# A gated delta rule's block inverse on one core: trimmed join products, and the second coupling as 32-column products in a packed operand

## The reference

```python
gc = jnp.cumsum(g, axis=-1)
decay = jnp.exp(jnp.where(causal, gc[..., :, None] - gc[..., None, :], -jnp.inf))
kb = k * beta[..., None]
a = jnp.where(strict, jnp.einsum('bhnid,bhnjd->bhnij', kb, k) * decay, 0.0)
rhs = jnp.concatenate([v * beta[..., None], kb * jnp.exp(gc)[..., None]], axis=-1)
sol = lax.linalg.triangular_solve(a + eye, rhs, left_side=True, lower=True)
u, w = sol[..., :dv], sol[..., dv:]
qk = jnp.where(causal, jnp.einsum('bhnid,bhnjd->bhnij', q, k) * decay, 0.0)
def step(state, inp):
    v_new = u_c - jnp.einsum('bhcd,bhde->bhce', w_c, state)
    o = jnp.einsum('bhcd,bhde->bhce', qd_c, state) + jnp.einsum('bhij,bhje->bhie', qk_c, v_new)
    state = state * cd_c[..., None, None] + jnp.einsum('bhcd,bhce->bhde', kd_c, v_new)
```

## Time and profile before

| | |
|---|---|
| Median of 3 runs | 2663.14 us (2659.54 to 8724.83) |
| The profiled execution's own time | 2661.84 us |
| Its span on the core | 2660.1 us |
| PE busy | 2594.3 us, 98% |
| Weight loads (PEld) | 2153.7 us, 81% |
| DVE busy | 1637.7 us, 62% |
| POOL busy | 1180.7 us, 44% |
| ACT busy | 1116.7 us, 42% |
| DMA, mean | 89 GB/s |
| TensorE's granted clock, mean | 0.995 |

### The profile page before, as it was taken

How to read it: one execution, slowest core, us unless ns; L and a number is a source line. 1 busy time by engine, 2 the same in 40 slices (tenths; PEclk the granted TensorE clock), 3 DMA queues, 4 the chain that set the end, 5 groups by cost and what they waited for, 6 DMA issues and landing times. The chain is left out here.

```text
span 2660.1 us, 34055 instructions
## 1 busy us (share of the span) xinstructions
PE 2594.3 (98%) x12821; PEld 2153.7 (81%) x12821; DVE 1637.7 (62%) x1743; ACT 1116.7 (42%) x1648; POOL 1180.7 (44%) x721
## 2 busy tenths in 40 slices
PE   7899999999999999999999999999999999999998
PEld 5788888888878888888888788888878888888887
DVE  5677666676177666665455657557557666665454
ACT  6445545545353443433344334434533434343242
POOL 2444333435313878774443111112413887874442
PEclk9999999999999999999999999999999999999999
DMA  3111011102342222224554111012521222224453
GB/s 121 30 43 47 32 41 46 47 32 73 95 146 78 87 72 96 72 95 159 180 173 137 58 32 48 24 55 70 166 98 64 87 84 84 80 99 155 171 189 115
DMA packets 84540, 238.06 MB, mean 89 GB/s; under 512 B 8928, under 2 KB 22816, under 8 KB 84416
## 3 DMA queue, kind: packets, MB, share of 16 engines
q1 hardware_dynamic: 84416, 236.39, 26.8%
HBM read 189.66 MB, written 46.69 MB: 89 GB/s over the span
## 5 line engine op out<-in xcount | busy, mean ns | idle before, releaser
L398 POOL TENSOR_TENSOR f_wlo<-f_raw,f_whi 128x512 fp32r<-128x512 f32 (+1 forms) x210 | 427.6, 2037 | 490.1 <-ACT f_whi L439 490.1
L712 DVE TENSOR_TENSOR f_hlo<-f_hraw,f_hhi 128x512 fp32r<-128x512 f32 x88 | 182.9, 2084 | 198.9 <-ACT f_hhi L497 198.9
L439 ACT ACTIVATE f_whi<-f_raw 128x512 fp32r<-128x512 f32 (+1 forms) x210 | 172.0, 834 | 269.2 <-PE f_value L82 252.2
L398 POOL TENSOR_TENSOR f_wlo<-f_sums,f_whi 128x512 fp32r<-128x512 f32 x144 | 188.5, 1319 | 39.8 <-ACT f_whi L439 39.8
L439 ACT ACTIVATE f_whi<-f_sums 128x512 fp32r<-128x512 f32 x144 | 90.4, 627 | 271.2 <-POOL f_sums L404 271.2
L80 PE MATMUL f_value<-x_hi,f_whi 128*128 128x512 f32 x416 | 162.7, 391 | 1.2 <-POOL f_wlo L398 1.2
L81 PE MATMUL f_value<-x_lo,f_whi 128*128 128x512 f32 x416 | 162.6, 391 | 0.0
L82 PE MATMUL f_value<-x_hi,f_wlo 128*128 128x512 f32 x416 | 162.5, 391 | 0.0
L80 PE MATMUL f_part<-f_whi,f_hhi 128*128 128x512 f32 x352 | 137.9, 392 | 0.0
L82 PE MATMUL f_part<-f_whi,f_hlo 128*128 128x512 f32 x352 | 137.5, 391 | 0.0
L81 PE MATMUL f_part<-f_wlo,f_hhi 128*128 128x512 f32 x352 | 137.1, 389 | 0.0
(11 more groups left out here) (539 smaller groups left out, 7649.0 us busy)
## 6 DMA issues: line engine op xcount, KB each, us to landing
f_raw<-in_ffn_w_up SPq DMA_DIRECT2D x88, 512.0 KB, 3.6
f_raw<-in_ffn_w_down SPq DMA_DIRECT2D x88, 512.0 KB, 3.6
hidden<-f_hid SPq DMA_DIRECT2D x44, 512.0 KB, 2.7
f_hraw<-hidden SPq DMA_DIRECT2D x88, 256.0 KB, 4.0
g_raw_first<-in_gdn_w_in SPq DMA_DIRECT2D x16, 512.0 KB, 3.6
g_raw<-in_gdn_w_in SPq DMA_DIRECT2D x16, 512.0 KB, 4.2
f_xt<-x_mid SPq DMA_DIRECT2D x16, 512.0 KB, 4.8
l_raw_first<-in_gla_w_in SPq DMA_DIRECT2D x12, 512.0 KB, 3.5
```

Source lines behind the costliest of these rows:

```text
L398: pool.tensor_tensor(part_of(w_lo, k), source, part_of(w_hi, k).bitcast(F32), ALU.subtract) \
L439: act.activation(part_of(w_hi, k), source, ACT.Copy).then_inc(s_hi, 1)
L712: dve.tensor_tensor(h_lo[d % FFN_SLOTS][:, :], h_raw[d % HIDDEN_RAWS][:, :], plain32(h_hi[d % FFN_SLOTS][:, :]), ALU.subtract).then_inc(s_ ...
```

## The change

Four things change, all in the joins.

- Join 0: `joined(0)` makes only 96 of the 128 rows of the inverse (`kept_rows`; the last 32 are needed by no later product), so its weight has 96 columns instead of 128, and DVE subtracts on 96 partitions. The moving operand keeps its 128 columns.
- Join 1, coupling: `coupled(1)` made 8 products of 128x128. It now makes 16 of 32x32 with 96 rows of contraction, one for each of the two pairs of 32-blocks (`PAIRS`), both in partitions 0 to 31 of `pm`. ACT copies them with 4 copies of 32x128 elements instead of 2 of 128x512, to the places (b, b) of `m1_low`, a view on `rowsT` of 64 columns for each chunk. What is between has to be zero, so POOL clears `m1_low` once per head (128x512), ahead of `coupling(h, 1)`; ACT waits for it on a new semaphore.
- Join 1, the join: `joined(1)` made 16 products of 128 columns with weights of 128 columns. It now makes 8 with weights of 64 columns and 32 moving columns, and 8 with weights of 64 columns and 64 moving columns. DVE's `join(1)` had 2 subtractions of 128x512 per half; it now has 3 of 32x128.
- Join 2: `coupled(2)` contracts over 64 rows instead of 128; its weight keeps 128 columns and its moving operand 64.

```diff
+        m1_low = rowsT[:, :].rearrange("p (c t) -> p c t", c=NT)
...
+        QUARTER = P // 4
+        PAIRS = [(slice(2 * b * QUARTER, (2 * b + 1) * QUARTER), slice((2 * b + 1) * QUARTER, (2 * b + 2) * QUARTER),
+                  slice(b * QUARTER, (b + 1) * QUARTER)) for b in range(2)]
+        kept_rows = slice(0, 3 * QUARTER)
...
                 spread(h, 1)
+                pool.memset(m1_low, 0.0).then_inc(s_zero, 1)
                 coupling(h, 1)
...
                     act.wait_ge(s_m1p, 2 * J * h + 2 * n + a + 1)
+                    if 0 < n < J - 1:
+                        if a == 0:
+                            act.wait_ge(s_zero, h + 1)
+                        for _, down, packed in PAIRS:
+                            last = act.activation(m1_low[down, part, packed],
+                                                  by_chunk(pm)[0:QUARTER, part, packed], ACT.Copy)
+                        last.then_inc(s_m1, 1)
+                        continue
...
-                    was, wasT = (inv, invT) if n else (first, firstT)
-                    dve.tensor_tensor(inv[:, part, :], was[:, part, :], x[:, 0], ALU.subtract)
-                    dve.tensor_tensor(invT[:, part, :], wasT[:, part, :], x[:, 1], ALU.subtract).then_inc(s_t, 1)
+                    if n:
+                        up, down, _ = PAIRS[0]
+                        dve.tensor_tensor(inv[down, part, up], inv[down, part, up], x[down, 0, :, up], ALU.subtract)
+                        for up, down, packed in PAIRS:
+                            last = dve.tensor_tensor(invT[up, part, down], invT[up, part, down],
+                                                     x[packed, 1, :, packed], ALU.subtract)
+                        last.then_inc(s_t, 1)
+                        continue
+                    dve.tensor_tensor(inv[kept_rows, part, :], first[kept_rows, part, :], x[kept_rows, 0],
+                                      ALU.subtract)
+                    dve.tensor_tensor(invT[:, part, :], firstT[:, part, :], x[:, 1], ALU.subtract).then_inc(s_t, 1)
...
                         if n == J - 1:
-                            last = pe.matmul(out[:, low], cT[:, c, :], x[:, c, low], start=True, stop=True)
+                            last = pe.matmul(out[:, low], cT[low, c, :], x[low, c, low], start=True, stop=True)
+                        elif n:
+                            for up, down, packed in PAIRS:
+                                last = pe.matmul(out[0:QUARTER, packed], cT[kept_rows, c, down],
+                                                 x[kept_rows, c, up], start=True, stop=True)
                         else:
-                            last = pe.matmul(out, (cT if n else near_cT)[:, c, :], x[:, c, :], start=True, stop=True)
+                            last = pe.matmul(out, near_cT[:, c, :], x[:, c, :], start=True, stop=True)
...
-                        pe.matmul(pt[:, at:at + P], xT[:, i, :], m1[:, i, :], start=True, stop=True)
+                        if n:
+                            pe.matmul(pt[low, at:at + QUARTER], xT[:, i, low], m1_low[:, i, 0:QUARTER],
+                                      start=True, stop=True)
+                            out = pt[low, at + HALF:at + HALF + P // 2].rearrange("p (b t) -> p b t", b=2)
+                            lower = xT[:, i, :].rearrange("p (b half t) -> p b half t", b=2, half=2)[:, :, 1, :]
+                            last = pe.matmul(out, m1_low[:, i, :], lower, start=True, stop=True)
+                            continue
+                        pe.matmul(pt[kept_rows, at:at + P], xT[:, i, kept_rows], m1[:, i, :], start=True, stop=True)
```

More of the change, by code:

```diff
@@ L1575, in gdn @@
         s_ct, s_m1p, s_m1 = sem("coupling_made"), sem("coupling_product_done"), sem("coupling_product_copied")
+        s_zero = sem("coupling_rows_zeroed")
         s_x, s_t = sem("join_products_done"), sem("blocks_joined")
```

## The result

The change makes the kernel slower: 2690.02 us in the median of four runs (2689.34 to 2691.81), against 2661.63 us for the kernel before on the same chip. The ratio is 1.0112, with a 95% interval of [1.0096, 1.0128]; it leaves out before's one slow run of 8724.83 us, without which before's median is 2660.12. So the change costs 30 us (28 against the median with that run), where I had expected 8 us less. I had forecast 2654, with a range up to 2664.

A forecast was written before the change was run, and what follows sets the result against it. PE bounds the kernel, with the gain capped by the start of DVE's second join. Seven heads at 0.96 us plus 1.5 for head 0 sum to 8.2 us, giving 2654 us; its own range 2651 to 2658, overall range 2648 to 2664.

The forecast's parts named there:

- The bound: PE, busy 98% of the span, counts; in front of the third coupling DVE's second join, starting at 339.96, caps the gain.
- the price of a narrow record: In `coupled(1)`, 0.067 us per record of a 32-column weight (bounds 0.033 and 0.118), making it 0.33 us longer.
- the line: Record price drawn through 0.113 us at 128 weight columns and 0.067 at 64, giving 0.044 at 32.
- rival B: `coupled(1)` ends early, POOL's `coupling(2)` precedes DVE's second tap, join 1.9 us later; 0.9 per head lost, 2668 us; chance 0.12.
- the proportion: Record cost going on in proportion to weight width: 0.033 us at 32 columns, half of 0.067.
- head 0: No fills there: `joined(1)` 1.35 us shorter, the 0.54 wait mostly gone, `coupled(1)` 0.33 longer; gain taken as 1.5 us.
- `joined(1)`: PE's products for join 1: 32 records with 64-column weights at 0.067, 2.14 us instead of 3.49.
- The third coupling: `coupled(2)` on PE: two halves of 0.92 us plus 0.1 for 32-row products and shape change, ending at 342.71 instead of 343.67.
- rival C: Array shape changes in `prepare` cost 0.3 us per border, not 0.09: 3 us in all, time 2658; chance 0.08.
- rival A: Narrow records cost 0.118 us: `coupled(1)` takes 3.78, 0.2 per head lost, time 2663.6; chance 0.12.
- DVE's pieces: Small subtractions of DVE's `join(1)`: 0.275 us each, neighbours overlapping by 0.08, three taking 0.67.
- Case D: `coupling(2)` lets DVE's third tap go first, so the join starts earlier: 1.4 us per head gained, 2651 us; chance 0.05.

## Why the prediction was wrong

**The bound.** That PE counts and that the join's start caps the gain was right, and it is what went wrong: the cap itself moved. I had its distance from the start of `coupled(1)` as constant, 8.3 us; it became 351.56 - 341.83 = 9.7.

**The step that failed: the price of a narrow record.** I took 0.067 us for a 32-column record, "since 64 columns already cost more than half of 128". It measured 1.13 / 32 = 0.035, next to the lower bound of 0.033 and below the line's 0.044. The floor of about 62 ns that the Trainium skill, TensorE: Matmul & The Clock Gate, section on 56 ns and 53.3 ns, gives for matmuls decoded by microcode is not what bounds these records; the other of its two, about 25 ns, is not contradicted. I had put the point where rival B decides at 0.047, and gave B 0.12 all the same. (Even that point was too low by my own numbers: over by 333.3 from a start at 331.64 is 1.66 / 32 = 0.052.) With both ends of the bound in hand and the deciding point between them, the chance of B had to follow from where in 0.033 to 0.118 the value may lie; two of the three ways to read it (the line and the proportion) lay on B's side.

**Rival B's size.** The mechanism was as written, in this order: POOL ahead of the second tap, two taps slowed, the join late. The join came 1.40 us later, where I had 1.9, and cost 0.72 per head with the clock up, where I had 0.9. B's 2668 counted seven such heads and a gain of 1.5 in head 0; the run with the wait filled measured 2672.9, with six such heads and losses in head 0, in the last head and behind it.

**The other step that failed, and the larger: the clock was in no case.** I let PE's idle time cost its own length. It cost 2.98 us per head on top of the join's 0.72, and six times 2.98 is 17.9 of the 30 us; from after to the run with the wait filled the time fell by 17.2 (2690.02 to 2672.86). The page of before showed a clock of 0.995 in the table, and I did not ask what holds it there. My range up to 2664 had no room for it. The kernels with the flip removed (2676, 2666, 2661) are above it or in its upper part for the same reason.

**The other terms.** `joined(1)`: 346.56 - 344.55 = 2.01, forecast 2.14. The third coupling, both halves with the shape changes: 1.97 with the clock up, forecast 1.94 (two halves and 0.1 for the changes), so rival C falls; rival A fell with the narrow record. DVE's pieces measured 0.28 each, as forecast, but don't overlap: three take 352.42 - 351.56 = 0.86, not 0.67. Over two halves that is 0.2 to 0.4 us, about the difference between the forecast's gain of 0.96 per head and what a head without a flip or a fall gained, 78.23 - 77.54 = 0.69; no run tested it alone. The MEMSET (0.52) costs nothing, as said; ACT's copies (four in 1.11 us, as forecast) lie under fill 20 in the loop. I had counted seven heads like head 3; head 7 is not one (67.58 us to its end in before). Head 0 was wrong in sign: a gain of 1.5 was forecast, and the stretch from its `coupled(1)` on became 2.2 us longer. ACT comes to its copies there only 3.01 us behind the start of `coupled(1)` (102.87 - 99.86), as in before (102.15 - 99.26 = 2.89), so what the narrow products save PE waits for, and behind that wait the clock falls for 10.2 us. With the waits filled the stretch is back at 74.88, against 74.59. The forecast's 77.3 per head was near, for a kernel in which neither the turn nor the clock moved.

**Case D** had a mechanism that exists: with the taps first and the wait filled a head gains 78.2 - 76.4 = 1.8 us, where I had 1.4. The change did not bring it about, since its product is released before the second tap, not behind the third.

## What to carry to other kernels

When a step gets shorter, ask what its end releases on other engines, and where in their queues that work will land; if the landing point is close to a border, work out the duration at which it crosses, and give the crossing the chance that the bounds give it. A short wait on PE is not priced by its length: look at the granted clock behind each of its waits, and fill one that can't be removed with matmuls whose result nobody reads. An order that holds only because two ends happen to fall right deserves a wait that fixes it.

## What the runs showed of the hardware

- **Narrow products.** Plain fp32 records with a 32-column weight and 32 moving columns and 96 rows come every 0.035 us, against 0.067 at a weight of 64 columns and 0.113 at 128. From 128 down to 32 the price falls with the weight's width. (At 32 the moving operand is as narrow as the weight, so that row can't tell the two apart; at 128, halving the moving columns changed nothing.) The number of rows does nothing: the third coupling's halves are alike with 64 and with 128.
- **POOL and DVE take turns by whole operations.** Behind one of POOL's, an operation of 8 columns took 1.59 us, and 2.18 behind `coupling(2)`; a tap took 3.15 instead of 1.28. A shift of 0.85 us in when POOL's product is queued (2.61 against 3.46 behind the gated output) moved the join by 1.40. The Trainium skill, GPSIMD Engine Reference, Key points, names the shared interface and, by that rule, the traces agree; the size of it is from these rows.
- **The clock falls for short waits.** PE idle for 1.42 us on full-width products was followed by the half clock in four of six heads; 1.55 us with the narrow products, in all; 0.31 to 0.48 us with the narrow products, in three of six, in two different kernels; 0.44 us in two pieces with full-width products, in none, and with their rows trimmed in one; narrow products with the wait filled, in none. In head 0 the clock fell for 10.2 us in all six kernels with narrow products and a wait of 2.4 us behind them, and in none of the four with full products, full rows and a wait of 1.5. I take from this that idle time alone can bring a fall and that narrow products beside it make one more likely. That is a reading of counts from one execution each, not a rule: why one head falls and its neighbour, with the same instructions, does not is open, and so is whether products over fewer rows count as well. The last head shows how loose it is: with the same waits of 1.4 and 2.3 us on full-width products there, the clock fell in before and not in before with the taps first.
- **What a fall costs.** In the loop heads the clock is back by itself after 3.4 or 6.8 us. A fall of 3.4 us cost 1.5 us (81.2 against 79.65, 77.9 against 76.4), and one of 6.8 us cost 3.0 (81.93 against 78.95). In after all six are of 6.8 us, behind a wait of 3.0; behind 1.55 us four were short and two long. Filling the wait cost nothing that shows (a period of 76.4, as in the heads without a fall), and no loop head fell in any of the three kernels where it was done.
